# Moving the start of matmul operands by 64 bytes in SBUF, in a two-layer hybrid backbone

## The reference, cut to what matters

```python
for l in range(DEPTH):
    need_ctx = l < DEPTH - 1
    ...
    hc = ada_ffn_half(hc, mc[0], mc[1], mc[2], ffn1_norm[l], ffn1_w_gu[l], ffn1_w_down[l])
    hx = ada_ffn_half(hx, mx[0], mx[1], mx[2], ffn1_norm[l], ffn1_w_gu[l], ffn1_w_down[l])
    uc = modulate(rms_norm(hc, mix_norm[l]), mc[3], mc[4])
    ux = modulate(rms_norm(hx, mix_norm[l]), mx[3], mx[4])
    yc, yx = token_mixing(uc, ux, ...)
    hx = hx + mx[5] * yx
    hx = ada_ffn_half(hx, mx[6], mx[7], mx[8], ffn2_norm[l], ffn2_w_gu[l], ffn2_w_down[l])
    if need_ctx:
        ...
return hx
```

## Time and profile before

| | us |
|---|---|
| median of three runs | 2533.5 |
| lowest and highest run | 2532.74, 2536.25 |
| span of the profiled execution | 2531.9 |

### The profile page before, as it was taken

The page is one execution under the profiler, slowest core; times in us unless marked ns, Lnnn a source line. Parts: engine busy times, 40 slices in busy tenths (PEclk is TensorE's granted clock), DMA queues, the critical chain, the costliest instruction groups (busy, mean ns, idle before and its releaser), DMA issues.

```text
span 2531.9 us, 37811 instructions
## 1 busy us (share of the span) xinstructions
PE 2430.3 (96%) x15806; PEld 2061.2 (81%) x15806; DVE 1466.0 (58%) x2287; ACT 945.7 (37%) x1537; POOL 90.4 (4%) x122
## 2 busy tenths in 40 slices
PE   5999999999989999999999999999999989999999
PEld 4888877867878888888888788888886878898999
DVE  5877656355667465577655453333354667567555
ACT  2322223365554422232222232322245554444543
POOL 0000000000023000000000000000000003100000
PEclk9999999999999999999999999999999999999999
DMA  7544543201200143335454332222321220055454
GB/s 274 215 181 185 183 150 114 87 34 51 84 35 2 34 166 124 126 117 200 183 199 166 150 110 100 100 96 98 107 100 67 84 84 2 19 177 173 167 184 167
DMA packets 44663, 309.65 MB, mean 122 GB/s; under 512 B 5072, under 2 KB 6224, under 8 KB 7632
## 3 DMA queue, kind: packets, MB, share of 16 engines
q1 hardware_dynamic: 44208, 305.98, 33.5%
q10 hardware_dynamic: 288, 1.27, 0.1%
HBM read 306.18 MB, written 1.05 MB: 121 GB/s over the span
## 4 chain that ended last, share of the span: by engine, by line
PE 89%; DVE 5%; ACT 3%; issue 2%; DMA 1%; SPq 0%; POOL 0%; ACTq 0%; DVEq 0%
PE bank L1475 74%; PE bank L1841 7%; PE bank L1468 2%; PE bank L1778 1%; PE bank L1757 1%; DVE w_lo L2097 1%; DVE u_lo L2144 1%; DVE sq L2136 1%; PE bank L1506 1%; ACT w_hi L933 1%; PE bank L1691 1%; DMA mod_par<-in_mod 0%; PE bank L1518 0%; PE bank L1766 0%; ACT work L1246 0%
## 5 line engine op out<-in xcount | busy, mean ns | idle before, releaser
L2097 DVE TENSOR_TENSOR w_lo<-ring,w_hi 128x1024 fp32r<-128x1024 f32 x420 | 510.5, 1224 | 676.5 <-ACT w_hi L933 671.7
L1475 PE MATMUL bank<-u_hi,w_hi 128*128 128x512 f32 (+1 forms) x2272 | 816.7, 359 | 27.9 <-DVE w_lo L2097 14.9
L1475 PE MATMUL bank<-u_hi,w_lo 128*128 128x512 f32 (+1 forms) x2272 | 805.8, 355 | 0.0
L1475 PE MATMUL bank<-u_lo,w_hi 128*128 128x512 f32 (+1 forms) x2272 | 805.3, 354 | 0.0
L933 ACT ACTIVATE w_hi<-ring 128x1024 fp32r<-128x1024 f32 x420 | 442.9, 1059 | 837.7 <-PE bank L1475 824.1
L1475 PEld LDWEIGHTS bank<-u_hi,w_hi 128*128 128x128 f32 x2272 | 432.9, 191 | 95.6 <-issue 21.6
L1475 PEld LDWEIGHTS bank<-u_lo,w_hi 128*128 128x128 f32 x2272 | 433.0, 191 | 59.4
L1475 PEld LDWEIGHTS bank<-u_hi,w_lo 128*128 128x128 f32 x2272 | 433.3, 191 | 56.8
L1475 PE MATMUL bank<-hidden_hi,w_hi 128*128 128x512 f32 (+1 forms) x722 | 260.6, 361 | 0.0
L1475 PE MATMUL bank<-hidden_lo,w_hi 128*128 128x512 f32 (+1 forms) x722 | 259.9, 360 | 0.0
L1475 PE MATMUL bank<-hidden_hi,w_lo 128*128 128x512 f32 (+1 forms) x722 | 259.9, 360 | 0.0
(11 more groups left out here) (236 smaller groups left out, 2458.1 us busy)
## 6 DMA issues: line engine op xcount, KB each, us to landing
ring<-in_wts SPq DMA_DIRECT2D x288, 1024.0 KB, 4.8
h<-in_x SPq DMA_DIRECT2D x8, 256.0 KB, 4.1
par<-in_par ACTq DMA_DIRECT2D x2, 620.0 KB, 6.0
out<-h SPq DMA_DIRECT2D x8, 128.0 KB, 4.2
cst<-in_cst SPq DMA_DIRECT2D x1, 704.0 KB, 11.8
mod_par<-in_mod SPq DMA_DIRECT2D x1, 96.0 KB, 12.0
cond<-in_c SPq DMA_DIRECT2D x1, 8.0 KB, 1.8
```

The lines of the kernel that those rows point to most:

```text
L1475: last = weights.used(pe.matmul(out, lhs[a], rhs[b], start=start and n == 0, stop=stop and n == 2))
L2097: tt(w_lo[:, b % HALVES, :], half_source(n % RING, part), w_hi[:, b % HALVES, :].bitcast(F32), ALU.subtract).then_inc(panel_left[n % RING] ...
```

## The change

Blank space is put in at two places; no instruction is added or removed. Only start addresses change:

- u_hi and u_lo get chunks of 544 columns (2176 bytes) where they had 512 (2048 bytes).
- A tile of 64 bytes is put ahead of the arena. With the 2048 bytes by which u_hi and u_lo grow together, the arena starts 2112 bytes later, at 129920, a multiple of 128.
- In the last layer's mixing and second feed-forward, the operands u (both parts), hidden (both), m (both) and y_hi are written and read 16 columns (64 bytes) later in their chunks. y_lo is not.

```diff
+LATER = 16
+U_PITCH = T + 2 * LATER
+
+def narrow(l):
+    return LATER if l + 1 == DEPTH else 0
...
-        u_hi = sb("u_hi", [P, DC, T], F32R)
-        u_lo = sb("u_lo", [P, DC, T], F32R)
+        u_whole_hi = sb("u_hi", [P, DC, U_PITCH], F32R)
+        u_whole_lo = sb("u_lo", [P, DC, U_PITCH], F32R)
...
         SLOT = T * 4
+        sb("ahead_of_arena", [P, 16])
         base = -(-nc.sbuf_base // 32) * 32
         sb("arena", [P, 48 * T])
...
+        def normed_chunks(l, i):
+            o = narrow(l) if i else 0
+            return [x[:, :, o:o + T] for x in (u_whole_hi, u_whole_lo)]
+
+        def hidden_chunks(l, f):
+            o = narrow(l) if f else 0
+            return [x[:, :, o:o + (SEQ if o else T)] for x in (h_whole_hi, h_whole_lo)]
+
+        def merged_chunks(l):
+            o = narrow(l)
+            return [x[:, :, o:o + (SEQ if o else T)] for x in (m_whole_hi, m_whole_lo)]
+
+        def branch_chunks(l):
+            o = narrow(l)
+            return [x[:, :, o:o + (SEQ if o else T)] for x in y_whole_hi], y_whole_lo
...
+            u = normed_chunks(l, 2 * f)
...
-                hid = (h_hi, h_lo)
+                hid = hidden_chunks(l, f)
...
-
+                u, merged, (y_hi, y_lo) = normed_chunks(l, 1), merged_chunks(l), branch_chunks(l)
```

More of the change, by code:

```diff
@@ L437, in at @@
             return nc.alloc_sbuf_tensor_at(name, [P, n, T], dt, offset=base + slot * SLOT)
-        h_hi = at("hidden_hi", 0, FC, F32R)
-        h_lo = at("hidden_lo", FC, FC, F32R)
+        h_whole_hi = at("hidden_hi", 0, FC, F32R)
+        h_whole_lo = at("hidden_lo", FC, FC, F32R)
         sg = at("sg", 2 * FC, 2)
@@ L444, in backbone @@
         ya, yb, yc = at("ya", 36, 4), at("yb", 40, 4), at("yc", 44, 4)
-        m_hi = at("m_hi", 0, DC, F32R)
-        m_lo = at("m_lo", DC, DC, F32R)
+        m_whole_hi = at("m_hi", 0, DC, F32R)
+        m_whole_lo = at("m_lo", DC, DC, F32R)
         def view(at, n, w=T):
@@ L505, in backbone @@
         mtmp = sq[:, 0:2, :]
-        y_hi = [at(f"y{b}_hi", 24 + 4 * b, 4, F32R) for b in range(3)]
-        y_lo = [at(f"y{b}_lo", 36 + 4 * b, 4, F32R) for b in range(3)]
+        y_whole_hi = [at(f"y{b}_hi", 24 + 4 * b, 4, F32R) for b in range(3)]
+        y_whole_lo = [at(f"y{b}_lo", 36 + 4 * b, 4, F32R) for b in range(3)]
         ADA_SUMS = {"ffn": (ada_sum_ffn[:, :, :], rt[:, :, :]), "merge": (view(6, 2), view(14, 2))}
@@ L937, in norm @@
             def norm(l, i, h_key):
+                u_hi, _ = normed_chunks(l, i)
                 def square(part):
@@ L977, in ffn @@
                 h0 = FC * (2 * l + f)
+                h_hi, _ = hidden_chunks(l, f)
                 def pair(i):
@@ L1345, in _ @@
                 act.wait_ge(ya_ready, l + 1)
+                y_hi, _ = branch_chunks(l)
+                m_hi, _ = merged_chunks(l)
                 for b, y in ((0, ya), (2, yc)):
@@ L1587, in second_part @@
                         spread(l, i, 1)
-                streamed([bank_of(key) for key in keys], [part_of(l, i, part)[1] for part in range(n)], u, u_rest_ready,
+                streamed([bank_of(key) for key in keys], [part_of(l, i, part)[1] for part in range(n)], normed_chunks(l, i), u_rest_ready,
                          DC * PART_AT[l, i], second_part)
-            u = (u_hi, u_lo)
             def ffn(l, f, w, carry):
+                u = normed_chunks(l, 2 * f)
                 following = (l, 1) if f == 0 else (l + 1, 0) if l + 1 < DEPTH else None
@@ L2031, in _ @@
                     free_bank((l, "out", c))
-                streamed([bank_of((l, "out", c)) for c in range(2)], [slice(0, w)], (m_hi, m_lo), m_rest_ready, DC * l)
+                streamed([bank_of((l, "out", c)) for c in range(2)], [slice(0, w)], merged, m_rest_ready, DC * l)
                 for p in range(1, 3):
-                    std([(l, "out", 2 * p), (l, "out", 2 * p + 1)], w, (m_hi, m_lo), None, 0)
-                std([(l, "out", 6)], w, (m_hi, m_lo), None, 0)
+                    std([(l, "out", 2 * p), (l, "out", 2 * p + 1)], w, merged, None, 0)
+                std([(l, "out", 6)], w, merged, None, 0)
                 if len(PARTS[l, 2]) > 1:
@@ L2038, in _ @@
                     free_bank((l, "out", 7))
-                    last_product((l, "out", 7), w2, (m_hi, m_lo), [(k, k, k == 0) for k in range(DC)], (l, 2))
+                    last_product((l, "out", 7), w2, merged, [(k, k, k == 0) for k in range(DC)], (l, 2))
                 else:
-                    std([(l, "out", 7)], w, (m_hi, m_lo), None, 0)
+                    std([(l, "out", 7)], w, merged, None, 0)
                     sums(l, 2, 0)
@@ L2121, in norm @@
                 items = norm_items(l, i)
+                u_hi, u_lo = normed_chunks(l, i)
                 def inverse(part):
@@ L2222, in ffn @@
                 h0 = FC * (2 * l + f)
+                h_hi, h_lo = hidden_chunks(l, f)
                 def pair(i):
@@ L2623, in _ @@
                     dve.wait_ge(out_kept[d], outs_before(l, 4, d))
+                m_hi, m_lo = merged_chunks(l)
+                y_hi, y_lo = branch_chunks(l)
                 def y_rest(b, y, n):
```

## The result

The changed kernel takes 2547.95 us (median of 4 runs, 2544.2 to 2549.23), beside 2534.88 for the kernel before on the same chip (4 runs, 2532.74 to 2538.37): a ratio of 1.0047 with a 95% interval of 1.0033 to 1.0062. The forecast was 2512.3. The sign is wrong, and the time lies outside the range.

The account below looks back on a forecast made before the run. The prediction took TensorE, busy 96% of the span, to be the bound, through its split matmuls' start intervals. Terms 13.3 + 6.7 + 4.6 - 1.8 - 1.0 - 0.6 = 21.2 us gained, 2533.5 to 2512.3 us; range 2508 to 2524.

Parts of the forecast that it names:

- (5): Placements taken at nothing: last layer's hidden, m, y_hi; first-layer u at 512 columns, bounded at 14.2 us either way.
- (1): Arena moved onto a multiple of 128 bytes: 1986 matmuls of 512 columns, 6.7 ns each, 13.3 us gained.
- (2): u 64 bytes later in the last feed-forward: 1008 matmuls of 256 columns, 6.6 ns each, 6.7 us gained.
- The price of 6.6 ns: Gain claimed per 256-column matmul when its operand starts 64 bytes over a multiple of 128 instead of on it.
- (3): u 64 bytes later in the last mixing, gates and other 256-column products: 4.6 us gained, bounds 0 and 6.5.
- The weights moving against u in gmv: Last layer's gmv, u stationary, 96 matmuls: taken at nothing, bound 0.6 us either way.
- (4): Operands moved the wrong way: last mixing's 264 matmuls of 512 columns lose 1.8 us, halves 1.0, y_lo 0.6.
- The halves: Halves of `last_product`, 256 columns of hidden and m, follow the arena onto the multiple: 156 matmuls, 1.0 us lost.
- The period is longer than 128, and the new residues are bad: Rival for u, hidden, m, y_hi: slower, 2538.1 us at one step of 6.7 ns, 2558 at two; chance 0.09.
- The address is not the cause: Rival: tensor or region, not address, sets the intervals; nothing follows the shift, no change, 2533.5 us; chance 0.08.
- The weight supply takes the last layer's gain: Rival: last-layer gains of (2) and (3) vanish into weight waits, 2523.6 us; chance 0.08 including partial following.
- the three signs of being wrong: Arena's 512 columns still at 233.4 ns; odd and even chunks differing; waits of L933 and L2097 growing by the matmuls' gain.

Follow-up runs that it names:

- e1: Kernel before with only u's chunk pitch raised to 2176 bytes, arena at its old residue: 2560.43 us, ratio 1.0100.
- e4: Kernel before with u's pitch of 2176 bytes and 1024 bytes between u_hi and u_lo, restoring their distance to a multiple of 2048: 2557.49 us, ratio 1.0089.
- e3: Kernel before with u's old pitch, u_lo 1024 bytes later against u_hi, arena at its old residue: 2536.45 us, ratio 1.0006.
- e11: Kernel before with u_hi alone in chunks of 2304 bytes, a multiple of 256: 2534.44 us, ratio 0.9999.
- e6: Kernel before with u_hi and u_lo both 128 bytes later, chunks of 2048 bytes, arena at its old residue: 2562.43 us, ratio 1.0105.
- e7: Kernel before with the weights w_hi and w_lo 64 bytes later, all other tiles at their old residues: 2560.61 us, ratio 1.0101.
- e10: Kernel before with the weights 192 bytes later, everything else at its old residue: 2533.53 us, ratio 0.9989.
- e2: Kernel before with only the 64 bytes ahead of the arena, u as before: 2529.16 us, ratio 0.9973.
- e5: Kernel before with the arena 64 bytes later, but the last layer's hidden, m and y at their old addresses: 2522.94 us, ratio 0.9951.
- e8: e5, with u of the last feed-forward also 192 bytes later in its chunks: 2518.52 us, ratio 0.9939.
- e12: e5, with u also read 64 bytes earlier from the last layer's mixing on: median 2517.21 us, ratio 0.9916.
- e16: The program of e9 unchanged, run once more: 2514.02 us, beside 2535.25 for the kernel before.
- e14: The program of e9 unchanged, run once more: 2526.37 us, beside 2535.25 for the kernel before.
- e15: The program of e12 unchanged, run once more: 2515.62 us, beside 2535.25 for the kernel before.
- e9: e5, with u of the last feed-forward also 64 bytes later in its chunks: 2522.27 us, ratio 0.9947.

## Why the prediction was wrong, step by step

**The step that failed is (5)**, "u in the first layer at 512 columns stays on a multiple of 128, by its pitch", taken at nothing. Its bound of 14.2 us stood in the text and was left out of the range; it was too small as well, since it counted the odd chunks alone. By the starts of the matmuls in the trace, even chunks (place 0) take about 233 ns and odd ones (place 128) 231, where all chunks at 0 take 226.7 and all at 128 take 232.5. All 4224 matmuls are slower, by 232.1 - 226.9 = 5.2 ns on the mean: **22 us lost**. e1 and e4 show it alone, e3 excludes the distance between u_hi and u_lo, e11 excludes a pitch as such.

Behind it stands a failed reading. The trace of before has only the places 0 and 192 of a period of 256, and by 128 these are 0 and 64. That the intervals are 17, 17.5, 9 and 8.5 times 32 cycles, "which speaks for 128 as the period", was no evidence: it is a property of durations, and says nothing of unseen addresses. e6 shows the period (u at 128 loses 6 ns), e7 and e10 what it is counted from. The reading "By the declarations u and the weights start on a multiple of 128 bytes" even named the weights, but took each address for itself.

The other terms, as (matmuls) x (difference of the mean intervals of contiguous matmuls, before and after):

- (1) Arena at 512: forecast 13.3 us gained; 1986 x (233.3 - 226.8) = **12.9**. Right; e2, e5 and e10 show it apart.
- (2) u at 256, last feed-forward: forecast 6.7; 1008 x (120.0 - 116.7) = **3.3**. The pitch puts chunks at 64 and 192 in turn. With one place for all, e8 has 113.4, the forecast value, which e12 at the same place missed. The price of 6.6 ns itself held only for one of two paces, so a full hit here would have been partly luck.
- (3) u at 256, last mixing: forecast 4.6; the interval went from 119.8 to 117.3, **2.2** gained. The weights moving against u in gmv, taken at nothing, went from 119.8 to 114.2: **0.5** gained.
- (4) u at 512 in the last mixing: forecast 1.8 lost; 264 x (230.0 - 227.0) = **0.8**. The halves: 1.0 forecast, **0.6** measured.
- (5) Last layer's hidden, m and y at nothing: they stay 64 bytes over a multiple of 128, but go from place 192 to 64 (y_lo to 0, the 0.6 of (4)). Hidden 528 x 4.4 ns = **2.3** lost, m **0.4**, y with y_lo 288 x 4.4 = **1.3**. As e16 has 113.3 ns at place 64, 117.8 is the slower of two paces there, and some or all of these 4.0 us can be the draw of a pace; m had half of its matmuls at 117.8 before already.

Sum: 22.0 + 0.8 + 0.6 + 2.3 + 0.4 + 1.3 - 12.9 - 3.3 - 2.2 - 0.5 = 8.5 us lost, of 10.5 in the span. (The first layer's gmv, 120.0 to 118.9 ns, gave 0.2 more.) The rest is granted clock. With the two traces laid matmul by matmul, some 7.3 us of the difference lie where both executions have the same clock and 3.0 where they have different ones. The largest such stretch is where the second layer's first feed-forward starts. Both kernels have a pause of TensorE of some 2 us there, and then the products go on. In windows of TensorE alone, first the changed kernel, with the pause in the first row:

```profile
1488.00:1494.00 6.00, 3.99 (x27) 0.93 0.53 176
1494.00:1500.00 6.00, 6.00 (x29) 0.50 0.01 3
```

and the kernel before, 6 us earlier in its trace:

```profile
1482.00:1488.00 6.00, 4.00 (x31) 1.00 0.51 179
1488.00:1494.00 6.00, 5.49 (x45) 1.00 0.00 1
```

After the same pause the granted clock was 0.50 in the one (1.2 GHz) and 1.00 in the other (2.4 GHz), and 29 matmuls follow in 6 us instead of 45. This feed-forward's gate and up products end 7.6 us later against their start than before, those of the feed-forward ahead of it, with no such row, 5.2: a difference of 2.4 us. The change need not have a part in this: e14 and e16 are one program and differ in the same way at the same stage, first e14, then e16:

```profile
1480.00:1490.00 10.00, 9.86 (x57) 0.66 0.10 38
1480.00:1490.00 10.00, 9.17 (x71) 1.00 0.00 1
```

Over the whole run the mean clock is 0.983 after and 0.987 before in the profiled executions.

**The rivals.** "The period is longer than 128, and the new residues are bad" is the one that came, given 0.09: 2538.1 us at one step, 2558 at two, and 2547.95 came. Its mechanism was right but for what the place is counted from. (Its "decides from 7.1 ns on" is mis-worked: with its own terms the 5.1 us are reached at 6.8 to 6.9 ns.) "The address is not the cause" fell with e2. "The weight supply takes the last layer's gain" fell too: at the faster pace e8 takes in 199 GB/s in a window without a wait, where u at 256 columns had 182, and TensorE's idle time before its u products that ends with w_lo is 15.0 us before (9.4 at 512 columns, 5.6 at 256) and 14.9 after (9.2 and 5.7). Of the three signs of being wrong that the text gave, one came: odd and even chunks differ. The arena's 512 did not stay at 233.4, and the waits for the weights did not grow.

**The range.** The text set 14.2 us as an unknown of either sign, called it "the range's widest bound", and then built the range without it. Taken in, the upper end would have been 2526.5, and with the 22 us that were measured, 2534: still short of the result. The missing part is the chance: two observed residues left half of all places unseen, and that is worth more than 0.09.

## What to carry to other kernels

Two addresses in a trace give two prices and no period; before an edit puts operands at places that no row shows, run one kernel that has only that placement. For split products in which TensorE never idles, lay the moving operand at 0 modulo 256 bytes from the stationary weights for 512 columns and at 192 (or 64, by e16) for 256, with a pitch that is a multiple of 256 bytes; here that was worth 0.84% (e12). At 256 columns count on 117.8 ns in place of 120.0, and take 113.4 as a chance. A price from one stretch of a trace is worth checking on all stretches with the same placement. An unmoved tensor can change its pace when the other operand is moved, so count both when tiles ahead of it change size.

## What the runs showed of the hardware

- The interval between matmuls of split products depends on the place of the moving operand against the stationary one, modulo 256 bytes: 226.7, 229.1, 232.5 and 233.3 ns for 512 columns at 0, 64, 128 and 192 (e11, e10, e6, before and e7). e7 and e10 change the interval of operands that were not moved.
- The Trainium skill, "SBUF — State Buffer", Who interferes with whom, has the matmul's moving operand and the weight load on two read ports of TensorE that are independent. By that rule e7 would have changed nothing; hidden went from 113.4 to 118.7 ns at 256 columns, and u at 512 from 226.7 to 233.2. The measurement decides; by what the two reads meet was not found.
- Chunks that alternate between 0 and 128 take 233 and 231 ns (after, e1, e4), the mean of 232.2 being that of 128 alone (232.5); 0 alone has 226.7.
- At 256 columns, at places 64 and 192, there are two steady paces, 113.4 and 117.8 ns, and one program can have either (e12 and e15, e9 and e16), as can one operand within one execution (m in the kernel before). In the last feed-forward, with its some 1,000 u matmuls and 528 of hidden, that is up to 1536 x 4.4 = 6.8 us between executions: the last piece of the chain takes 188.64 us in e12 and 181.77 in e15.
- The granted clock differs between executions of one program as well. e14 and e16, one program, lie 12.4 us apart. The last piece of the chain, first of e14, then of e16, holds 4.8 of them, 1008 x 4.5 ns = 4.5 us being the pace of u:

```profile
2332.78 189.15 PE bank L1513 x1584
2325.24 184.31 PE bank L1513 x1584
```

  The 7.5 us ahead of that piece lie, matmul by matmul, in the stretches where the two have different clocks (mean 0.981 in e14, 0.988 in e16); where both have the same, nothing is lost.
